# Modulation columns in four chunks, with keys, values and two index query tiles accumulated between them

## What is computed

```python
mod = silu(c) @ w_ada + b_ada                 # 1024 x 3072
shift, scale, gate = split(mod, 3)
h = rmsnorm(x, norm_gain) * (1.0 + scale) + shift
proj = h @ w_in                               # keys, values, queries, index queries, gates ...
```

## Time and profile before

| | us |
|---|---|
| median of 3 runs (846.28 to 846.84) | 846.73 |
| the profiled execution | 845.77 |
| its span in the trace | 843.7 |
| PE busy in the span | 803.9 |
| DVE, ACT, POOL busy | 569.6, 350.9, 381.0 |
| first product of keys and values starts | 40.47 |
| first product of the late index query tiles starts | 81.38 |

### The profile page before, as it was taken

How to read it: one execution, slowest core, us unless ns; L and a number is a source line. 1 busy time by engine, 2 the same in 40 slices (tenths; PEclk the granted TensorE clock), 3 DMA queues, 4 the chain that set the end, 5 groups by cost and what they waited for, 6 DMA issues and landing times.

```text
span 843.7 us, 13949 instructions
## 1 busy us (share of the span) xinstructions
PE 803.9 (95%) x4978; PEld 707.9 (84%) x4978; DVE 569.6 (68%) x1193; ACT 350.9 (42%) x647; POOL 381.0 (45%) x333
## 2 busy tenths in 40 slices
PE   3899999999999999999999999999998899999998
PEld 3699998889998888887788877788887787889998
DVE  5845538978988888888889536556666775754332
ACT  6473346665222222233232223778776773320000
POOL 1024544335624468852652212766888512982200
PEclk9899999999999999999999999999999999999999
DMA  9930110004432320230123223633433014744322
GB/s 344 380 87 17 51 50 15 26 13 125 132 94 63 100 86 18 97 113 25 50 88 101 99 88 124 227 113 113 127 111 96 18 24 147 250 134 135 122 93 74
DMA packets 62685, 87.95 MB, mean 104 GB/s; under 512 B 5881, under 2 KB 44317, under 8 KB 61726
## 3 DMA queue, kind: packets, MB, share of 16 engines
q1 hardware_dynamic: 48606, 64.04, 24.1%
q10 hardware_dynamic: 12096, 16.78, 5.5%
q0 software_dynamic: 1920, 6.29, 2.0%
HBM read 66.12 MB, written 20.97 MB: 103 GB/s over the span
## 4 chain that ended last, share of the span: by engine, by line
PE 84%; DVE 4%; ACT 4%; DMA 3%; issue 2%; SPq 1%; POOL 0%; DVEq 0%; ACTq 0%
PE pp L679 23%; PE pp L680 22%; PE pp L681 22%; PE pp L992 4%; PE pt L972 3%; PE ps L817 3%; PE ps L816 3%; DMA ada_w<-in_w_ada 2%; DVE prob L1997 1%; DVE score L1852 1%; ACT pT L1360 1%; DVE pT L1939 1%; ACT w_hi L616 1%; SPq L489 1%; ACT a_out L1310 1%
## 5 line engine op out<-in xcount | busy, mean ns | idle before, releaser
L621 POOL TENSOR_TENSOR w_lo<-w_raw,w_hi 128x1024 fp32r<-128x1024 f32 x50 | 123.7, 2492 | 217.1 <-ACT w_hi L616 165.1
L1876 DVE TENSOR_SCALAR_CACHE_REDUCE junk<-score,cand 128x384 uint8<-128x384 f32 (+1 forms) x186 | 168.6, 944 | 19.3 <-issue 13.3
L679 PE MATMUL pp<-hT_hi,w_hi 128*128 128x512 f32 x384 | 150.2, 391 | 0.0
L681 PE MATMUL pp<-hT_hi,w_lo 128*128 128x512 f32 x384 | 149.5, 389 | 0.0
L680 PE MATMUL pp<-hT_lo,w_hi 128*128 128x512 f32 x384 | 149.4, 389 | 0.0
L679 PE MATMUL pp<-w_hi,hT_hi 128*128 128x256 f32 x352 | 101.2, 287 | 0.5 <-ACT zb_out L1175 0.5
L681 PE MATMUL pp<-w_hi,hT_lo 128*128 128x256 f32 x352 | 99.4, 282 | 0.0
L680 PE MATMUL pp<-w_lo,hT_hi 128*128 128x256 f32 x352 | 99.4, 282 | 0.0
L1939 DVE TENSOR_TENSOR pT<-pt,pT 128x512 fp32r<-128x512 f32 (+3 forms) x96 | 50.6, 555 | 56.0 <-ACT pT L1360 53.1
L679 PEld LDWEIGHTS pp<-hT_hi,w_hi 128*128 128x128 f32 x384 | 72.1, 188 | 16.2 <-issue 0.8
L681 PEld LDWEIGHTS pp<-hT_hi,w_lo 128*128 128x128 f32 x384 | 72.1, 188 | 15.2
(11 more groups left out here) (275 smaller groups left out, 1819.9 us busy)
## 6 DMA issues: line engine op xcount, KB each, us to landing
w_raw<-in_w_in SPq DMA_DIRECT2D x36, 512.0 KB, 3.7
ada_w<-in_w_ada SPq DMA_DIRECT2D x7, 1024.0 KB, 11.6
sgb_spill<-stage ACTq DMA_DIRECT2D x16, 256.0 KB, 2.0
sga_spill<-stage ACTq DMA_DIRECT2D x16, 256.0 KB, 2.0
stage<-sga_spill SPq DMA_DIRECT2D x16, 256.0 KB, 3.1
ma_spill<-stage POOLq DMA_DIRECT2D x16, 256.0 KB, 2.4
gate_w<-in_w_ada SPq DMA_DIRECT2D x16, 256.0 KB, 2.8
w_raw<-in_w_out SPq DMA_DIRECT2D x8, 512.0 KB, 4.2
```

Of the source, the lines that this page charges most:

```text
L621: nc.gpsimd.tensor_tensor(lo, raw, hi.bitcast(F32), ALU.subtract).then_inc(w_lo_done, 1)
L679: nc.tensor.matmul(o, a_hi, b_hi, start=first, stop=False)
L681: return nc.tensor.matmul(o, a_lo, b_hi, start=False, stop=last)
L1876: v.tensor_scalar(junk[:, n % 2, 0:keys(b)], score[:, score_at(b):score_at(b + 1)], least, None, ALU.is_ge, ALU.add, accum_out=cnt[:, n:n ...
```

## The change

- SP loads w_ada in four chunks instead of eight rows. Chunk p holds, for all eight rows, 256 columns of `shift` and 256 of `scale`: what the contraction blocks 2p and 2p+1 need. Pieces 2 to 5 of w_in stand between the chunks, x tiles 4 to 7 behind them. Chunks 2 and 3 reuse the buffers of chunks 0 and 1 and wait for both their readers.
- Of chunk p PE takes the rows in `PE_ROWS[p]` (`ada_columns`), DVE the others (`ada_fold`), and PE adds DVE's sum (`ada_total`). DVE writes `shift` and `gmul` for the two blocks (`ada_finish`).
- ACT applies them while reading the transpose bank, and then rounds; POOL subtracts `hT_lo` for the first half.
- PE runs pair by pair: keys and values of blocks 2p and 2p+1 (`kv_step`), the next two transposes, columns and total of the next chunk, then the same two blocks of the index query tiles 2 and 3 (`early_step`, now 512 columns wide, over both halves of the query weights).
- Keys and values of four tiles share one accumulator pair of banks, and ACT drains them at once.
- The squares and scalings of x are divided between ACT and DVE. The sine and cosine work of DVE moves between the steps of the second half. `keep_warm` runs eight times at the start and no more before and after the totals.

```diff
-    EARLY = [(0, 2), (0, 3), (1, 2), (1, 3)]
+    EARLY = [2, 3]
...
+    PAIRS = KD // 2
+    PE_ROWS = [[0, 1, 4, 5, 6], [0, 4, 5, 6], [4, 5], [4, 5]]
...
+            def load_ada(p):
+
+                if p >= 2:
+                    sp.wait_ge(ada_sum, p - 1)
+                    sp.wait_ge(ada_used_p, p - 1)
+                for r in range(2):
+                    for part in range(2):
+                        sp.dma_start(ada_rows(p)[:, 4 * r:4 * r + 4, part * CW:(part + 1) * CW],
+                                     ada[:, 4 * r:4 * r + 4, part * D + p * CW:part * D + (p + 1) * CW]).then_inc(ada_in[p][r], 16)
             load_piece(0)
             load_piece(1)
-            for k in range(KD - 1):
-                sp.dma_start(ada_w[:, k, :], ada[:, k, 0:2 * D]).then_inc(ada_in[k], 16)
...
             load_piece(2)
-            load_x(4)
-            load_x(5)
+            load_ada(0)
             load_piece(3)
-            load_x(6)
-            load_x(7)
+            load_ada(1)
             load_piece(4)
+            load_ada(2)
+            load_piece(5)
+            load_ada(3)
+            for t in range(NT // 2, NT):
+                load_x(t)
...
+            def ada_columns(p):
+
+                if p >= 2:
+                    pe.wait_ge(mod_read, p - 1)
+                for r in PE_ROWS[p]:
+                    pe.wait_ge(ada_in[p][r // 4], 32)
                     for j in range(4):
-                        last = rows_step(o[j], 4 * f + j, ci, k, KR_W)
...
+                        last = nc.tensor.matmul(mod_column(p, j), ada_rows(p)[:, r, j * P:(j + 1) * P], c_silu[:, r:r + 1],
+                                                start=(r == PE_ROWS[p][0] and j == 0), stop=False)
+                last.then_inc(ada_used_p, 1)
+
+            def ada_total(p):
+
+                pe.wait_ge(ada_sum, p + 1)
+                for j in range(4):
+                    last = nc.tensor.matmul(mod_column(p, j), ada_acc[:, p % 2, j * P:(j + 1) * P], ones[:, 0:1],
+                                            start=False, stop=(j == 3))
+                last.then_inc(mod_full, 1)
...
+            for p in range(PAIRS):
+                pe.wait_ge(w_lo_done, 1 if p < PAIRS // 2 else 2)
+                kv_step(both, 0, 2 * p)
+                kv_step(both, 0, 2 * p + 1)
+                h_transposes(2 * p + 2)
+                h_transposes(2 * p + 3)
+                if p + 1 < PAIRS:
+                    ada_columns(p + 1)
+                    ada_total(p + 1)
+                early_step(2 * p)
+                early_step(2 * p + 1)
...
+                if f == 0:
+                    o = pt_take(("h", n))
+                    act.wait_ge(gmul_ready, k // 2 + 1)
+                    nc.scalar.activation(xT[:, k, :], o[:], ACT.Identity, scale=gmul[:, k:k + 1],
+                                         bias=shift[:, k:k + 1]).then_inc(pt_free_a, 1)
+                    act.wait_ge(pt_free_a, pt_done[pt_at[("h", n)]][0])
...
+            for p in range(PAIRS):
+                ht_lo(2 * p)
+                ht_lo(2 * p + 1)
+                if p < 2:
+                    pool.wait_ge(w_lo_done, 4 + p)
+                    split_piece_lo(pool, 4 + p)
...
+            def ada_fold(p):
+
+                acc, rows = ada_acc[:, p % 2, :], ada_rows(p)
+                own = [r for r in range(KD) if r not in PE_ROWS[p]]
+                for r in own:
+                    dve.wait_ge(ada_in[p][r // 4], 32)
+                    if r == own[0]:
+                        ins = v.tensor_scalar(acc, rows[:, r, :], c_silu[:, r:r + 1], None, ALU.mult)
+                    else:
+                        ins = v.scalar_tensor_tensor(acc, rows[:, r, :], c_silu[:, r:r + 1], acc, ALU.mult, ALU.add)
```

More of the change, by code:

```diff
@@ L542, in _ @@
             first_wa = pieces_through[name_of[("wa", 0)] - 1]
-            for n in range(5, first_wa + 4):
+            for n in range(6, first_wa + 4):
                 load_piece(n)
@@ L706, in yb_transposes, with keep_warm @@
                 last.then_inc(pt_full if b >= YB_PT else pp_full, 1)
+            def keep_warm(n):
+                for _ in range(n):
+                    nc.tensor.matmul(pp[1][:], ident_b[:], prefix[:, 0:512], start=True, stop=True)
             pe.wait_ge(consts, 1)
+            keep_warm(8)
             pe.wait_ge(dve_ready, V_POS)
@@ L728, in _ @@
             modulation = ps_claim("ada")
-            def keep_warm(n):
-                for _ in range(n):
-                    nc.tensor.matmul(pp[1][:], ident_b[:], prefix[:, 0:512], start=True, stop=True)
-            def ada_columns(k, first, end):
-                for j in range(first, end):
-                    nc.tensor.matmul(modulation[:, k * ADA_COLS + j:k * ADA_COLS + j + 1], ada_w[:, k, j * P:(j + 1) * P],
-                                     c_silu[:, k:k + 1], start=True, stop=True)
@@ L739, in _ @@
-            pe.wait_ge(c_silu_done, 1)
-            pe.wait_ge(ada_in[0], 16)
-            ada_columns(0, 0, ADA_COLS)
-            for n in range(KD):
-                h_transposes(n)
-            keep_warm(12)
-            for i in range(4):
-                pe.wait_ge(ada_sum, i + 1)
-                for j in range(4 * i, 4 * i + 4):
-                    last = nc.tensor.matmul(modulation[:, ADA_PE * ADA_COLS + j:ADA_PE * ADA_COLS + j + 1],
-                                            ada_acc[:, j * P:(j + 1) * P], ones[:, 0:1], start=True, stop=True)
@@ new lines, in early_step @@
+            def early_step(k):
+                pe.wait_ge(w_lo_done, 4 if k < 4 else 6)
+                for t in EARLY:
+                    o = pp_claim(("qi2", t)) if k == 0 else pp[pp_bank[pp_at[("qi2", t)]]]
+                    tok = slice(t * P, (t + 1) * P)
+                    last = product(o[:], hT_hi[:, k, tok], hT_lo[:, k, tok], w_hi[:, :, k, :], w_lo[:, :, k, :],
+                                   k == 0, k == KD - 1)
+                    if k == KD - 1:
+                        last.then_inc(pp_full, 1)
@@ L1734, in _ @@
[L1734 to L1744 removed]
+            dve.wait_ge(c_silu_done, 1)
@@ L1745, in _, with trig_angles @@
+            ada_fold(0)
+            ada_finish(0)
+            split_piece_v(3)
+            for p in range(1, PAIRS):
+                ada_fold(p)
+                ada_finish(p)
+            dve.wait_ge(mod_read, PAIRS)
+            dve.sem_inc(ps_free_v, 1)
+            square(6)
+            square(7)
             mean_half(1)
             rsqrt_half(1)
-            for n in range(KD, 2 * KD):
-                k = n % KD
+            scale(6)
+            scale(7)
+            def trig_angles():
+                for k in range(NF):
+                    v.tensor_scalar(angle[:, :, k], pos_col[:], float(np.float32(THETA ** (-2.0 * k / ROT))), None, ALU.mult)
+                dve.drain()
```

325 lines of the change are left out of this document (153 added, 172 removed).

## The result

The changed kernel is slower: 859.96 us in the median of four runs (856.54 to 860.69) against 846.50 for the kernel before on the same chip, ratio 1.0155 with a 95% interval of 1.0124 to 1.0185. Forecast were 855.6 and a range of 848.5 to 862.5. One execution each of the last two kernels of this document (1587.81 and 2768.40 us) was slow, two to three times as long as the others, and no ratio counts them.

The account below looks back on a forecast made before the run. TensorE, busy 95% of the span, was taken to bound the kernel. Stage sum +5.9, port +1.5 and clock +2.0 gave +9.4 us: 855.2 profiled, about 855.6 as median, range 848.5 to 862.5.

Parts of the forecast that it names:

- What bounds, and that a shift goes through unchanged: TensorE, busy 95% of the span, bounds; a shift of the first late query product goes nearly unchanged to the end.
- The load and the first product: w_ada loads at 350 GB/s, chunk 0's columns run at 1.2 GHz; keys and values start at 31.5, 9.0 earlier.
- the sum: TensorE's stage times up to the late query tiles added up: they start at 87.3 against 81.38, +5.9 us.
- From there to the second half: First product to second half: products, transposes, columns, stalls and starting low clock, 41.5 us; port 1.5 and clock 2.0 extra.
- the wait of about 1 us per pair: Sign expected in the changed kernel's profile: TensorE waits about 1 us for `hT_lo` in each pair.
- The clock term: Column blocks of chunks 1 to 3 drop TensorE's clock one or two times out of three chances; 2.0 us.
- The port term: First half: VectorE's folds and GpSimd's `hT_lo` subtractions take turns; 0 to 3.5 us for all pairs, taken as 1.5.
- Keys and values of the second half: Stretch before the late tiles stays at 14.3 us; trigonometry moved there finds VectorE idle time, bounds 0 and 1.
- The first columns run at 2.4 GHz: Rival: `keep_warm` keeps the clock up for chunk 0, 8.1 us less than +5.9, so -2.2, 844.5; chance 0.10.
- Only the sum: Rival: the clock holds and the port hides, so only +5.9 us, 852.6; chance 0.23.
- Much slower: Rival: every column block drops the clock and fold 2 holds the total up; +14.4, 861.1; chance 0.12.
- The overlap of the pairs: Rival doubted it: chunk 3 lands at 50, wanted at 60; shows only if that slack of 10 were gone.

Follow-up runs that it names:

- the last two kernels of this document: k3 and m1, the two versions of the best arrangement found; 845.96 and 846.46 us.
- m1: k3 with TensorE taking three rows of chunk 0, VectorE five, and the trigonometry split over VectorE's idle times; 846.46 us, ratio 1.0015.
- f1: Changed kernel with 28 column matmuls instead of 60, VectorE folding the rest and subtracting first-half hT_lo, plus moved splitting, squares and trigonometry; 856.87 us, ratio 1.0140.
- e2: Changed kernel with one column matmul instead of 16, 8 and 8 for chunks 1 to 3 (computation left out); 850.91 us, ratio 1.0060.
- after: The changed kernel itself, against the kernel before; 859.96 us, ratio 1.0155.
- h1: Changed kernel with the edits of e1 and e2 together (most columns of chunks 1 to 3 left out, trigonometry early); 848.19 us, ratio 1.0032.
- e1: Changed kernel with VectorE's sine and cosine work put back ahead of the second half; 856.21 us, ratio 1.0125.
- the first experiment: The run e1: changed kernel with VectorE's trigonometry back ahead of the second half; 856.21 us, ratio 1.0125.
- e3: Changed kernel with VectorE folding one row of chunks 1 to 3 instead of four to six (computation left out); 858.52 us, ratio 1.0157.
- e4: Changed kernel with constant matmuls added on TensorE at the start and around chunk 0's columns and total; 856.15 us, ratio 1.0114.
- c1: e1 with hT_lo of the first half subtracted by VectorE behind each chunk's ada_finish instead of by GpSimd; 861.48 us, ratio 1.0205.
- k1: e1 with the first two rows of chunk 1's columns moved into TensorE's wait ahead of the first product; 852.21 us, ratio 1.0082.
- k3: e1 and k1 together, fewer column rows on TensorE, x tiles 4 to 7 squared by ScalarE; 845.96 us, ratio 1.0005.

## Why the prediction was right, and where it was off

*What bounds, and that a shift goes through unchanged.* Right: 14.36 at the late tiles, 14.1 in the span, and 761.2 to 762.6 us behind them in eleven of the thirteen changed kernels (763.4 in m1, 765.7 in f1).

*The load and the first product.* Right. The load ran at 350 GB/s from 14 to 30 us, the value that the sum took. The columns of chunk 0 began at 16.55 and took 0.213 us an instruction, 1.2 GHz (8.67 for 40). First product 32.02 for 31.5; the wait for `hT_lo` after the total was 3.49.

*From there to the second half: 41.5, and 3.5 for port and clock, 45.0 in all.* Measured 46.4. By stages: keys and values 13.4 (10.7 and 2.4 for the low clock); transposes 4.0 (3.5); columns and totals 11.0 (9.9); the wait for x 1.47 (1.1); the early steps 16.6, where the sum had 10.9 of work, 3.0 of stalls, 1.5 of port and 2.0 of clock, 17.4. The total of these four terms came close. Their division was wrong: TensorE had no stall there at all in the profiled execution, and the wait of about 1 us per pair that the prediction names as a sign did not show. Stalls and slow clock lie on top of each other, which the sum had allowed for with "less the stall that it fills". One wording of the sum is wrong: the 5.6 us that cover the scaling of x are two early steps, a stall and two key steps; two key steps alone are 2.7.

*The clock term, 2.0, one or two falls.* There were three, 13.6 us long together. Two pairs of kernels measure what falls cost net, with the 6.5 us of the columns taken off: 2.3 us for three falls (e2 against after), 1.5 for two (h1 against e1: 8.0 between first product and late tiles). Of these, 1.2 and 0.4 belong to the clock ahead of the first block, which the sum has in its 2.4 for the start. Left are 1.1 in both pairs, half of the 2.0: more falls than the sum took and each at a lower price, because the waits that come back are nearly as large as what a fall costs.

*The port term, 1.5.* Right as a mechanism (the median fold was 1.62 us instead of 0.75; a pair of subtractions 2.95 to 3.38 instead of 2.6), not borne out as a cost: folding almost nothing gained 1.4 us by the medians, within the spread of after, and nothing by the ratios.

*Keys and values of the second half: 14.3, bounds 0 and 1 for the trigonometry.* This is the step that failed. It took 17.3, and the first experiment gave all of it back. The sum had weighed the length of the moved steps against VectorE's idle time and bounded them by 1. It had not asked what stands behind each of them: `h_raw` of the next block, which three engines want in turn, so that even the 2.5 us of the steps' own length were not free. And it had not asked what each of them meets: the port term was applied to the folds of the first half alone, although GpSimd subtracts every odd block of the second half as well. Two steps caught beside a subtraction made it 4.5 us. That the place of the steps cost 3.1 is shown; how the 3.1 divides between the port and their own length is not. The Trainium skill ("SBUF — State Buffer", section "Who interferes with whom") has the rule in a form that covers this: a `tensor_scalar`, though it reads one tensor, can also take the port pair that VectorE shares with GpSimd, and whoever is second is blocked for the whole of the other instruction. The trace agrees: 1.32 us for a step of 0.23.

The misses are 0.5 at the first product, 1.4 in the first half and 3.0 in the second: 4.9 of the 5.0 between +9.4 and +14.4. None of the three balances another. Inside the first half, though, terms do: in the early steps the clock took some 5 us (16.6 less four times the 2.8 of the last pair) where the sum had 2.0, and stalls and port nothing where it had 4.5. That their total came within 0.8 us is in part luck.

*The rivals.* "The first columns run at 2.4 GHz" fell: 0.213 us each, and with TensorE kept busy the grant held for only 4.5 us of columns. "Only the sum" fell with the three falls. "Much slower" (+14.4, 861.1) lies nearer to the measured 859.96 than the forecast does (1.1 against 4.4), but by a wrong account: every block did drop the clock, but fold 2 did not hold up a total, and the rest came from the second half. The overlap of the pairs worked; chunk 3 was never waited for.

Open is what exactly drops the grant. Of 15 blocks of 24 instructions (columns and total) behind the first product (after, e1, e3, e4, c1, k1, k3, m1), 11 saw it fall during the block or within a microsecond; which ones do changes from one profile to the next, and none of the six short groups of 10 (e2, h1) did. All five blocks of 40 did (after, e1, e3, e4, c1).

## What to carry to other kernels

Before a phase is split so that its consumers can start earlier, list what had been hidden beside the old wait (here transposes, totals and columns, some 12 us of TensorE) and price it as visible; an early start of 8.4 us did not pay for it even with columns and clock free. Look at the granted clock and the pitch, not only at busy time and brackets: a gapless TensorE timeline held 13.6 us at half speed, and the cure is to put the thin work into waits that exist anyway rather than among dense products. When a step is moved into an engine's idle time, check what is queued behind it there and who waits for that, and what the other engine on the same port does in that very slot.

## What the runs showed of the hardware that I had not expected

- Column matmuls let the clock fall although TensorE is busy all the time (3.41 of 3.41 us from 38.25, then 0.50 from 41.66), and without them no fall came (e2, h1). The kernel before had one such fall; that nearly every block would bring one I had not expected. The Trainium skill ("TensorE: Matmul & The Clock Gate", section "HAM oscillation — how this bites in real kernels") warns of idle gaps between bursts; here there was none.
- Mixed with products, the same columns kept the clock low for 18.4 us, where the products alone brought it back in 5.5. Two dense constants behind every eight column instructions did not hold it (20.97).
- Four runs of one kernel can lie 4.5 us apart (e4: 853.97 to 858.46), while ten of h1, without column blocks, lie within 1.3 (847.64 to 848.90). These runs do not show that the blocks are the reason: e1 has them and lies within 0.5, and the kernel before spreads over 4.0.
